# A mixture-of-experts decoder step: the last two experts' rows reach their tokens by 0/1 products instead of through memory

## What is computed

```python
x = _layer_norm(ALPHA * x + mix @ w_out, ln1_g, ln1_b)
x = _layer_norm(ALPHA * x + _moe(x, ...), ln2_g, ln2_b)

def _moe(x, ...):                      # 16 experts in 4 groups
    probs = softmax(xt @ w_router + b_router)
    ...                                # top-1 group, then top-2 experts in it
    wts = vals / jnp.sum(vals, -1, keepdims=True)
    gate = jnp.sum(jax.nn.one_hot(idx, N_EXPERTS) * wts[..., None], axis=1)
    h = silu(xt @ w_e_gate[e]) * (xt @ w_e_up[e])      # for every expert e
    h = h * gate[..., None]
    return jnp.einsum('nef,efd->nd', h, w_e_down)
```

## Time and profile before

| | |
|---|---|
| median of 3 runs | 899.3 us (898.61 to 899.36) |
| profiled execution | 900.57 us, its span 899.3 us, granted clock 0.99 |
| TensorE busy | 867.6 us, 96% of the span |
| VectorE, ScalarE, GpSimd busy | 360.5, 206.3, 85.6 us |
| last up product of expert 15 ends | 849.1 us |
| last down product copied by ScalarE | 862.20 us |
| last output transfer issued | 893.03 us |

### The profile page before, as it was taken

One profiled execution on the slowest core, in us unless ns is written; L12 is line 12 of the kernel. 1 busy time (PEld: TensorE's weight loads), 2 busy tenths in 40 slices (PEclk: granted clock), 3 DMA queues, 4 the chain that ended last, 5 costly groups with the idle time before them and its releaser, 6 DMA issues.

```text
span 899.3 us, 20975 instructions
## 1 busy us (share of the span) xinstructions
PE 867.6 (96%) x9437; PEld 710.4 (79%) x9437; DVE 360.5 (40%) x749; ACT 206.3 (23%) x313; POOL 85.6 (10%) x89
## 2 busy tenths in 40 slices
PE   7999999999999999999999999999999999999964
PEld 6999888898989999999999988666666566565631
DVE  5653645736575372233232555722311211111146
ACT  4521141311422332322221201231111111111112
POOL 1210000000000001001101021400001000100053
PEclk9999999999999999999999999999999999999987
DMA  9895171492816043222221923699999999999566
GB/s 323 268 286 152 48 264 65 146 313 64 280 48 211 1 156 93 84 67 87 94 95 47 378 102 151 243 371 400 401 404 405 398 410 411 406 404 424 215 210 125
DMA packets 85374, 203.47 MB, mean 226 GB/s; under 512 B 4237, under 2 KB 57189, under 8 KB 76472
## 3 DMA queue, kind: packets, MB, share of 16 engines
q1 hardware_dynamic: 78216, 177.17, 53.5%
q0 software_dynamic: 7088, 25.26, 9.1%
HBM read 172.58 MB, written 32.06 MB: 228 GB/s over the span
## 4 chain that ended last, share of the span: by engine, by line
PE 91%; DMA 4%; DVE 2%; ACT 1%; issue 1%; POOL 0%; SPq 0%; DVEq 0%; POOLq 0%
PE psum L2159 18%; PE psum L465 17%; PE psum L467 17%; PE psum L466 16%; PE psum L2173 9%; PE psum L1863 2%; DMA xg<-x_rows,idx_i 2%; PE psum L1873 2%; PE psum L2146 2%; PE psum L1902 1%; PE psum L2105 1%; PE psum L2072 1%; DMA ya_rows<-y_slots,dest_i 1%; DMA xn<-in_x_prompt_dram 1%; PE psum L1888 1%; PE psum L2037 1%
## 5 line engine op out<-in xcount | busy, mean ns | idle before, releaser
L465 PE MATMUL psum<-x_hi,split_lo 128*128 128x272 f32 x704 | 208.9, 297 | 2.0 <-DVE pbl L1427 1.2
L467 PE MATMUL psum<-x_hi,split_hi 128*128 128x272 f32 x704 | 202.3, 287 | 0.0
L466 PE MATMUL psum<-x_lo,split_hi 128*128 128x272 f32 x704 | 202.1, 287 | 0.0
L2159 PE MATMUL psum<-set,xt 128*32 128x256 f32 x3072 | 169.1, 380 | 0.0
L2159 PEld LDWEIGHTS psum<-set,xt 128*32 128x32 f32 x3072 | 98.2, 110 | 65.7 <-issue 2.4
L465 PEld LDWEIGHTS psum<-x_hi,split_lo 128*128 128x128 f32 x704 | 132.6, 188 | 7.3 <-issue 2.7
L466 PEld LDWEIGHTS psum<-x_lo,split_hi 128*128 128x128 f32 x704 | 132.8, 189 | 1.4 <-issue 1.0
L467 PEld LDWEIGHTS psum<-x_hi,split_hi 128*128 128x128 f32 x704 | 132.6, 188 | 0.0
L460 DVE TENSOR_TENSOR split_lo<-raw,split_hi 128x2048 fp32r<-128x2048 f32 x35 | 80.0, 2290 | 113.8 <-ACT split_hi L441 113.3
L2173 PE MATMUL psum<-set,hT 128*32 128x256 f32 x1536 | 86.2, 380 | 1.5 <-DVE ys L1651 1.5
L2173 PEld LDWEIGHTS psum<-set,hT 128*32 128x32 f32 x1536 | 49.0, 110 | 32.8 <-ACT hT L1051 1.7
(11 more groups left out here) (355 smaller groups left out, 1250.3 us busy)
## 6 DMA issues: line engine op xcount, KB each, us to landing
set<-in_w_e_gate_dram SPq DMA_DIRECT2D x32, 1024.0 KB, 18.3
set<-in_w_e_up_dram SPq DMA_DIRECT2D x32, 1024.0 KB, 20.9
set<-in_w_e_down_dram SPq DMA_DIRECT2D x32, 1024.0 KB, 21.2
raw<-in_w_in_dram SPq DMA_DIRECT2D x26, 1024.0 KB, 6.5
cb<-in_state_C_dram SPq DMA_DIRECT2D x8, 1024.0 KB, 7.9
out_dram<-cb SPq DMA_DIRECT2D x8, 1024.0 KB, 5.8
y_slots<-ys POOLq DMA_DIRECT2D x15, 384.0 KB, 7.3
y_slots<-x_hi POOLq DMA_DIRECT2D x3, 1536.0 KB, 14.8
```

Of the source, the lines that this page charges most:

```text
L465: nc.tensor.matmul(out, a_lo, b_hi, start=first, stop=False)
L466: nc.tensor.matmul(out, a_hi, b_lo, start=False, stop=False)
L467: return nc.tensor.matmul(out, a_hi, b_hi, start=False, stop=last)
L2159: last = mm(gate_up()[32 * b:32 * b + 32, j], xt[:, kk, 32 * mine:32 * mine + 32], w, start=kk == 0 and j != 1, stop=kk == KT - 1 and j > 0)
```

## The change

- The gathers of both choices start when the rows of expert 13 are stored. Experts 14 and 15 are no longer stored; their rows of y_slots are filled with zeros early in the kernel, so that a gathered row of theirs adds nothing. The zeros come from the constants, by four transfers on SP after the bias rows; the one zero store of GpSimd for expert 15 goes.
- Rows of 14 and 15 stay in SBUF. ScalarE multiplies them with each slot's gate into a rounded high part (high_part, fp32r), VectorE makes the low part, what is left of the product (low_part). A 0/1 matrix of 96 slots by 544 tokens for each of the two experts (oh14, oh15) sends them to their tokens: add_late makes four fp32r products of 512 columns for each tile and expert.
- The 0/1 matrices and the gate of each slot come from late_slots on VectorE, after turn 4; the gate is split into three bf16 parts in choice_gates (named) and found by the same products that find the slot's token.
- Second choices are added to x1 by VectorE (add_second) in tiles 0, 2, 3 and 4. In tile 1 TensorE still adds them by the diagonal matrix, the only one that is left.
- In the last turn the transposes of hs stand between the two halves of down 14; the hidden columns go to hT_last and the last down product to banks 6 and 7 (results_last). ScalarE takes all copies of expert 14, and the 96x768 part of 15.
- The loading of the block count and the branch on it come after the ending on each engine; the branch gets its own form of the ending.

The diff, cut to its core:

```diff
@@ sync
+                sp.wait_ge(cst_in, 16)
+                for e in (NE - 2, NE - 1):
+                    for c in (0, 512):
+                        sp.dma_start(y_slots[e * CAP:(e + 1) * CAP, c:c + 512], const("head_sel")[32:32 + CAP, 0:512]
+                                     ).then_inc(zero_out, 16)
...
-        sp.wait_ge(ya_ok, NE)
-        sp.dma_start(y_slots[(NE - 1) * CAP:NE * CAP, 0:512], ys[1][0:CAP, 0:512]).then_inc(last_out, 16)
-        sp.wait_ge(yd_ok, NE)
-        sp.dma_start(y_slots[(NE - 1) * CAP:NE * CAP, 512:DM], ys[1][0:CAP, 512:DM]).then_inc(last_out, 16)
+        sp.wait_ge(np_ok, 1)
...
+        sp.wait_ge(outs, 16 * NT)
+        sp.wait_ge(cp_out, 16 * H)
         sp.wait_ge(xa_ok, 1)
         extra = sp.value_load(ctl[0:1, XTRA:XTRA + 1], min_val=0, max_val=XTRA)
@@ gpsimd
-        for e in range(NE - 4, NE - 1):
+        for e in range(NE - 4, NE - 2):
             store_y(e)
...
+        pl.wait_ge(ys_out[0], 16 * (NE // 2 - 1))
+        pl.wait_ge(ys_out[1], 16 * (NE // 2 - 1))
+        for i in range(NT):
+            gather_rows(0, ya, i)
+        pl.wait_ge(gu_done, 2 * NE - 2)
+        for i in range(NT):
+            gather_rows(1, yb_, i)
@@ scalar
-        turn(NE - 1, True, True, y_used=(ys_out[0], 16 * (NE // 2 - 1)))
+        def high_part(q, b):
+            at = slice(512 * b, 512 * b + 512)
+            ac.wait_ge(ya_ok, NE - 1 + q)
+            if b:
+                ac.wait_ge(yd_ok, NE - 1 + q)
+            nc.scalar.activation(late_y[q][0][0:CAP, at], ys[q][0:CAP, at], ACT.Copy, scale=gslot[0:CAP, q:q + 1]
+                                 ).then_inc(act_rows, 1)
...
+        gate_sigmoid(2 * NE)
+        ac.wait_ge(hi_done, NE)
+        nc.scalar.copy(hT_last[:], psum[:, 6, 0:QB * P].rearrange("p (q t) -> p q t", q=QB)).then_inc(ht_ok, 1)
+        ac.wait_ge(ys_out[0], 16 * (NE // 2 - 1))
+        store_half(0, 2 * NE - 2)
+        nc.scalar.copy(ys[0][0:CAP, 512:768], psum[0:CAP, 5, 0:256])
+        for b in range(QB):
+            last = nc.scalar.copy(ys[0][b * 32:b * 32 + 32, 768:DM], fourth_columns(b))
+        last.then_inc(yd_ok, 1)
+        for b in range(2):
+            high_part(0, b)
...
+        nc.scalar.copy(ys[1][0:CAP, 0:768], results_last()[0:CAP, 0:768]).then_inc(ya_ok, 1)
+        for b in range(2):
+            high_part(1, b)
@@ vector
+        silu(NE - 1)
+        for i in range(2):
+            add_first(i)
+        add_first(2)
+        low_part(0, 0)
+        low_part(0, 1)
+        add_first(3)
...
+        for b in range(QB):
+            last = v.tensor_copy(ys[1][b * 32:b * 32 + 32, 768:DM], results_last()[CAP:P, 256 * b:256 * b + 256])
+        last.then_inc(yd_ok, 1)
+        add_second(0)
+        low_part(1, 0)
+        low_part(1, 1)
+        add_second(2)
...
+        stats(0)
+        for i in range(NT):
+            centred(i)
+            if i == 0:
+                add_second(3)
+            if i == 1:
+                add_first(PT)
+                add_second(PT)
+            if i < NT - 1:
+                stats(i + 1)
@@ tensor
-        turn(NE - 1, True, 8 * NE, 8 * NE, None)
+        down(0, 8 * NE, 0)
+        pe.wait_ge(hs_ok, NE)
+        hidden_in()
+        down(0, 8 * NE, 1)
         pe.wait_ge(ht_ok, NE)
-        pe.wait_ge(yd_ok, NE - 1)
-        pe.wait_ge(ya_ok, NE - 1)
         for half in range(2):
-            down(1, 8 * NE, half)
+            down(1, 8 * NE, half, hT_last, results_last)
...
+        def add_late(i, q, first=False):
+            r = ROWS[i]
+            pe.wait_ge(act_rows, HIGH[q][1])
+            pe.wait_ge(lo_y, 2 * q + 2)
+            for part in (1, 0):
+                for b in range(2):
+                    last = mm(summed(i)[0:r, b, :], late[q][0:CAP, P * i:P * i + r],
+                              late_y[q][part][0:CAP, b * 512:b * 512 + 512], start=first and part == 1, stop=q == 1 and part == 0)
+            if q:
+                last.then_inc(pc_ok, 1)
+
+        for i in range(2):
+            add_late(i, 0, True)
+        for i in range(2):
+            own_rows(i, False)
+            if i:
+                pe.wait_ge(dg_ok, 1)
+                pe.wait_ge(yb_in[i], 16)
+                for b in range(2):
+                    mm(summed(i)[:, b, :], diag[:, i, :], yb_[i][:, b * 512:b * 512 + 512], start=False, stop=False)
+            add_late(i, 1)
+        for i in range(2, NT):
+            own_rows(i)
+            add_late(i, 0)
+            add_late(i, 1)
```

## The result

| | before | after |
|---|---|---|
| median of five runs each | 899.3 us | 903.48 us |
| ratio, 95% interval | | 1.0058 (1.0039 to 1.0076) |
| profiled execution, span | 900.57 us, 899.3 us | 903.48 us, 902.3 us |

A forecast was written before the change was run, and what follows sets the result against it. It took the chain after the last expert as the bound: row stores, gathers, then an ending paced by VectorE. VectorE's new end at 884.4 plus 7.7 gave 892.1, plus 0.8 for SP 892.9 us, against 899.3; range 890.8 to 897.2.

The forecast's parts named there:

- Part 1: Last two experts on TensorE: transposes wait for nothing, last down product starts at 855.0, ends at 860.4, 1.8 us earlier.
- Part 2: Ending's gathers on GpSimd: start at 846.6 instead of 860.82, ten issued by about 861, landed by about 866.
- Parts 3 to 5: Late copies, adds, TensorE sums and endings: first statistics at 866.2 instead of 876.84, VectorE done at 884.4, end 892.1.
- Part 6: SP's block-count load and branch moved behind the outputs: 0.8 us taken, bounds 0 and 1.14, giving 892.9.
- Rival A: TensorE's clock falls anyway in the gap before tile 0's sums; VectorE ends 3.9 us later, 896.8; chance 0.11.
- Rival B: Second-choice gathers land up to 4.5 us later, making VectorE's adds wait 1 to 2 us: 894.5; chance 0.10.
- The rule of the Trainium skill's GPSIMD Engine Reference, Specifications: GpSimd shares SBUF interfaces with VectorE and contends with two-SBUF-input instructions: 0.9 us delay per gather issue, at most five times.
- Rivals C and D: Ending: C, TensorE becomes the bound at 1.2 GHz, 910.5, chance 0.06; D, output transfers bound, about 899, chance 0.03.

The follow-up runs named there:

- e1: Changed kernel without the ending's ten gathers, five plain copies of other rows made in the expert loop instead (wrong sums): 894.82 us, ratio 0.9944.
- e2: Changed kernel with one wait more: the gathers start only when the down product of expert 14 is done; 905.51 us.
- e3: Changed kernel with the ten gathers replaced by ten plain copies of as many rows (wrong rows), on GpSimd's queue 894.31 us, on SP's 895.1 us.
- e7: Changed kernel with ten gathers of 16 rows back to back, plain copies of the other rows behind all ten (wrong rows): 905.7 us.
- f2: Changed kernel with tile 4 last, tile 2's second choice added later, and one small GpSimd instruction between gathers, no landing waits: 895.93 us, ratio 0.9944.
- f3: Changed kernel with three gathers in flight in the ending, plus ten 16-row gathers back to back in the loop turn of expert 11: 908.06 us.
- e5: Changed kernel with each gather split: 16 rows by address, the others by a plain copy right behind it (wrong rows); 895.57 us.
- e8: Changed kernel with its ten full gathers, but row addresses in order instead of scattered (wrong rows): 904.62 us.
- e9a: Changed kernel with at most two gathers in flight, tile 4 last, tile 2's second choice added later on VectorE: 897.04 us, ratio 0.9962.
- e6a: Changed kernel with GpSimd waiting for each gather to land before the next, tile 4 last: 918.55 us, ratio 1.0195.

## Why the prediction was wrong

- **The step that failed** is in Part 1, that the transposes "wait for nothing" and the last down product starts at 855.0. It took the disturbance by the gathers at nothing without a reason. Part 2's "Nothing else is on the queues then" is true of the queues, but it shows how I had asked: what could delay the gathers, and what they could delay on the queues, not what they do to engines that wait for neither. They start at 847.44 (846.6 summed). They cost TensorE 9.8 us (15.6 - 5.8, with the lower clock behind the gaps in it), and the last down product starts at 864.73. A part of it would have been lost without any gap on TensorE: hs was ready at 852.73, 0.9 us behind the 851.8 at which the transposes were to start, since ScalarE was held up. This is shown by e1 (none, nothing lost), e2 (the gaps move with them), e3 (not the bytes, not GpSimd's queue as such) and e7 (small ones do the same).
- **Why before didn't show it.** This is argued, not tested. There the gathers lie where TensorE waits or runs few long products, and in the loop there is one per turn. The change moved the burst beside TensorE's most compact stretch. This also means that part of what I booked as free, an earlier start of the gathers, was the thing to be priced.
- **Parts 3 to 5 held** as pitches. Scaled copies 0.67 us each (0.65 taken), low parts 1.41 for two (1.4), a late expert 0.92 to 0.95 (0.94), the pitches of the statistics within 0.2 us. e1's span of 892.3 against a sum of 892.1 says the same, for the fastest of its six executions. That the sum on the span could stand for the median was a coincidence: in the five executions of the changed kernel the time is 1.2 to 1.4 us above the span, and only the kernel before had a profiled execution that was as much slower than its median. By the median e1 is 2.7 us above the 892.1.
- **Part 6** was too dear: from the last issue to the end of the span the changed kernel takes 902.3 - 896.01 = 6.3 us, before took 6.3. No run shows a gain from it. The term is 0, not 0.8.
- **Rival A** (the clock falls in the gap ahead of tile 0) did not happen: the granted clock is 1.00 from 864 to 891, the gap included. It was lower ahead of that, 0.56 from 860 to 862 and 0.58 from 862 to 864, as a consequence of the gaps in which TensorE had started three to nine products in two microseconds; that is in the 9.8. The sign that I had given for A or C, statistics released by TensorE by more than 0.5 us, was drawn too fine: it reads 0.56 here and 0.55 in e1, with neither. **Rival B** (second choices late) did not happen: the last gather was issued at 859.32, earlier than the sum had it, and no second-choice addition waited for one. The rule of the Trainium skill's GPSIMD Engine Reference, Specifications, which I had cited, is seen at up to 1.38 us for an issue against 1.0, with no effect on the end. In f2 it is larger: GpSimd's fillers take 0.57 to 1.6 us. **Rivals C and D** did not happen. None of my rivals was the true one: each asked what would make the gathers, the products or the outputs late, and none what the gathers do to engines that don't wait for them. The 0.07 that I had given to "slower" was for other mechanisms.
- **What is open** is the path. TensorE is held up in starting products and loads, ScalarE in starting its gate_sigmoid and its copy, with no semaphore and no port that the profile names. It looks like the delivery of instructions. The Trainium skill's Runtime: NRT & Kernel Launch, Instruction fetch mechanics, says that an engine's code comes in blocks of 16 KB by a transfer queue of its own, ahead of use. By that rule a delay would come once in hundreds of instructions; the trace has a gap after every three to five products, and its list of transfer queues has one instruction packet from 847 to 862 us (queue, kind: packets, MB, share of 16 engines):

```profile
q8 instruction: 1, 0.02, 0.6%
```

So the arrival of such packets doesn't explain gaps at every few products. In f3 the list from 710 to 820 us has no instruction packet at all, and TensorE loses 12.3 us there. Whether the issuing of gathers shares a path with the engines' sequencers, these runs can't show. For full gathers the number under way and the pace go together, at 1.3 us per issue and some 4 to 6 us to land; e7 separates them, and with some two small gathers under way it has the largest measure. So the pace of the issues fits all runs and the number of waiting gathers does not. Whether it is the pace as such, or that nothing else stands between two gathers on GpSimd, is not told apart: e5 and f2 change both. Spacing the gathers in the kernel before was not tried, so what spacing alone is worth there, without the change, is not known.

## What to carry to other kernels

Row-addressed gathers issued back to back by GpSimd can hold up the starting of instructions on TensorE and ScalarE, ScalarE from the second gather on, TensorE from the third or fourth, until up to 3 us behind the last issue. Ten of them cost about 1 us each, whatever they move. Where such a burst is moved beside a compact stretch of another engine, price it, or space it: with a wait for a landing that keeps two or three in flight, or one short GpSimd instruction between two gathers, this change was worth 0.4 to 0.6% where it had cost 0.6%. In a profile look for idle time with the sign "issue" inside a run of equal instructions, and for what another engine does over just that stretch.

## What the runs showed of the hardware

- Ten gathers at 1.14 to 1.32 us from start to start (means) cost TensorE 9.8 to 12.3 us (changed kernel, e7, e8, f3); ten plain copies of the same bytes on the same queue, at 0.53 us, cost nothing, with the transfer engines busy for the whole stretch.
- The number of gathers under way does not decide it: in e7 the rows of each have moved 2.3 us after its issue starts. ScalarE starts 1.26 us late with only two full gathers issued (e9a).
- It hits instructions of a loop body as well (f3), so having run before is no protection.
- A lone gather of 512 KB takes 4.40 to 5.97 us from issue to landing (e6a), but in the burst of the changed kernel they move 303 to 385 GB/s, by which I estimate one every 1.4 to 1.7 us. The Trainium skill's DMA: Bandwidth & Descriptors, Anatomy of one DMA — SWDGE (gpsimd) path, gives 2.0 us and the bytes at 436 GB/s; an estimate from that page would be 3.2 us, and the measurement decides. The same section says that many descriptors can be emitted before their cost shows. On GpSimd that agrees (0.8 to 1.0 us each beside a quiet VectorE, for 16 rows or 128); it showed on the other engines.
